# Where the adaptive norm's weight pieces stand in the two feed-forward blocks: 56 of 96 in the Down runs in place of 32

## The reference, cut to what matters

```
def _swiglu(h, w_gu, w_down):
    gate, up = jnp.split(h @ w_gu, 2, axis=-1)
    return (jax.nn.silu(gate) * up) @ w_down
...
    x = x + 0.5 * _swiglu(_rmsnorm(x, ffn1_norm), ffn1_w_gu, ffn1_w_down)
    x = x + _token_mixing(...)
    x = x + 0.5 * _swiglu(_rmsnorm(x, ffn2_norm), ffn2_w_gu, ffn2_w_down)
...
    c_act = jax.nn.silu(c)
    for l in range(2):
        mod = c_act @ w_ada[l] + b_ada[l]            # w_ada[l]: 2048 x 6144
        shift, scale, gate = jnp.split(mod, 3, axis=-1)
        h = _rmsnorm_2(x, norm_g[l]) * (1.0 + scale) + shift
```

## Time and profile before

| | us |
|---|---|
| median of 3 runs | 3013.56 |
| lowest, highest | 3011.37, 3015.36 |
| the profiled execution | 3013.77 |
| its span (first to last instruction) | 3012.0 |
| PE busy in it | 2990.2 |
| DVE, POOL, ACT busy | 2138.6, 1531.6, 1502.0 |
| first Down runs, PE's first matmul to the last | 490.85 to 730.7 |

### The profile page before, as it was taken

One profiled execution on the slowest core, in us unless ns is written; L12 is line 12 of the kernel. 1 busy time (PEld: TensorE's weight loads), 2 busy tenths in 40 slices (PEclk: granted clock), 3 DMA queues, 4 the chain that ended last, 5 costly groups with the idle time before them and its releaser, 6 DMA issues.

```text
span 3012.0 us, 48048 instructions
## 1 busy us (share of the span) xinstructions
PE 2990.2 (99%) x19120; PEld 2671.4 (89%) x19120; DVE 2138.6 (71%) x3446; ACT 1502.0 (50%) x1999; POOL 1531.6 (51%) x749
## 2 busy tenths in 40 slices
PE   8999999999999999999999999999999999999998
PEld 7888888888999999998888888888899998999997
DVE  4889886764324447787688887777579866789764
ACT  6555544444667455544555554444544454534454
POOL 5887764445565555585578876444550004710013
PEclk9999999999999999999999999999999999999999
DMA  6888887885776555566688888788576546666455
GB/s 217 288 278 271 278 280 247 305 288 181 229 176 176 158 165 148 151 171 201 200 284 282 266 281 287 242 306 277 173 216 194 162 147 216 181 190 182 154 182 181
DMA packets 491671, 663.43 MB, mean 220 GB/s; under 512 B 70440, under 2 KB 278040, under 8 KB 490936
## 3 DMA queue, kind: packets, MB, share of 16 engines
q1 hardware_dynamic: 485960, 655.85, 68.2%
q0 software_dynamic: 4448, 2.94, 0.4%
q10 hardware_dynamic: 1040, 1.58, 0.2%
HBM read 656.06 MB, written 2.11 MB: 219 GB/s over the span
## 4 chain that ended last, share of the span: by engine, by line
PE 95%; DVE 3%; ACT 1%; DMA 0%; issue 0%; POOL 0%; DVEq 0%; ACTq 0%
PE ps L1142 33%; PE ps L1006 20%; PE ps L1147 17%; PE ps L1012 10%; PE ps L1023 3%; PE ps L1175 2%; PE ps L1028 1%; PE ps L1171 1%; PE ps L990 1%; PE ps L1667 1%; DVE narrow_split_slabs L2261 1%; PE ps L1181 1%; PE ps L1443 1%; PE ps L1424 1%; PE ps L1178 1%; DVE h_split L2218 1%
## 5 line engine op out<-in xcount | busy, mean ns | idle before, releaser
L925 POOL TENSOR_TENSOR split_slabs<-stage,split_slabs 128x1024 fp32r<-128x1024 f32 x366 | 892.3, 2447 | 1005.4 <-ACT split_slabs L1723 999.4
L1723 ACT ACTIVATE split_slabs<-stage 128x1024 fp32r<-128x1024 f32 x544 | 573.4, 1059 | 558.3 <-PE ps L1147 435.8
L1723 ACT ACTIVATE narrow_split_slabs<-stage 128x1024 fp32r<-128x1024 f32 (+1 forms) x437 | 457.3, 1050 | 589.1 <-PE ps L1012 442.5
L1142 PE MATMUL ps<-split_slabs,h_split 128*128 128x512 f32 x2904 | 719.6, 390 | 0.8 <-ACT split_slabs L1723 0.8
L1142 PEld LDWEIGHTS ps<-split_slabs,h_split 128*128 128x128 f32 x2904 | 541.7, 188 | 111.4 <-ACT split_slabs L1723 1.2
L1006 PE MATMUL ps<-h_split,narrow_split_slabs 128*128 128x256 f32 x4928 | 620.6, 279 | 3.1 <-issue 1.9
L925 POOL TENSOR_TENSOR narrow_split_slabs<-stage,narrow_split_slabs 128x1024 fp32r<-128x1024 f32 (+1 forms) x182 | 441.2, 2434 | 315.8 <-ACT narrow_split_slabs L1723 315.5
L1006 PEld LDWEIGHTS ps<-h_split,narrow_split_slabs 128*128 128x128 f32 x4928 | 586.7, 188 | 13.0 <-issue 7.7
L2261 DVE TENSOR_TENSOR split_slabs<-stage,split_slabs 128x1024 fp32r<-128x1024 f32 x178 | 258.3, 1453 | 272.8 <-ACT split_slabs L1723 272.0
L2261 DVE TENSOR_TENSOR narrow_split_slabs<-stage,narrow_split_slabs 128x1024 fp32r<-128x1024 f32 x255 | 338.3, 1330 | 126.5 <-ACT narrow_split_slabs L1723 126.1
L1147 PE MATMUL ps<-split_slabs,h_split 128*128 128x512 f32 x1452 | 388.2, 389 | 0.0
(11 more groups left out here) (346 smaller groups left out, 3293.0 us busy)
## 6 DMA issues: line engine op xcount, KB each, us to landing
stage<-in_ffn_w_gu SPq DMA_DIRECT2D x352, 512.0 KB, 4.8
stage<-in_w_in SPq DMA_DIRECT2D x349, 512.0 KB, 3.7
U<-in_w_ada SPq DMA_DIRECT2D x192, 512.0 KB, 5.7
stage<-in_ffn_w_down SPq DMA_DIRECT2D x176, 512.0 KB, 5.2
stage<-in_w_out SPq DMA_DIRECT2D x96, 512.0 KB, 4.2
stage<-in_w_in SPq DMA_DIRECT2D x80, 128.0 KB, 2.9
stage<-in_w_branch_c SPq DMA_DIRECT2D x32, 192.0 KB, 3.4
stage<-in_cmp_w SPq DMA_DIRECT2D x8, 512.0 KB, 4.3
```

The costliest lines, as they stand in the source:

```text
L925: nc.gpsimd.tensor_tensor(slab_part(n, 1, size(n)), stage[:, n % RING, 0:size(n)], slab_part(n, 0, size(n)).bitcast(F32), ALU.subtract).th ...
L1142: mm(ps[:, 2 * pair + T, :], stationary(kk, i)[:, T * P:(T + 1) * P], w[0][:, kk, :], start=first and kk == 0 and i == 0, stop=False)
L1723: return fn(slab_part(n, 0, size(n)), stage[:, n % RING, 0:size(n)], ACT.Copy)
```

## The change

Of the 96 pieces of each block 40 stand in the gate and up run in place of 64, and 56 stand in Down in place of 32. In Down they stood at each odd slab from 9 to 71; now they stand at each slab from 9 to 71 that is not a multiple of 8. The first piece of all stays at slab 26 of the block and the last at Down's 71. From Down's slab 8 on, DVE keeps the low part of each fourth slab only (9, 13, 17, ... 85); 20 low parts of each block go from DVE to POOL, so that POOL has 65 of Down's 88 and DVE 23.

```diff
-ADA_EARLY = 64
+ADA_EARLY = 40
...
         by_vector |= set(summed)
+        by_vector -= {s + GU_SLABS + i for s in (S_F1, S_F2) for i in range(8, DOWN * DOWN_GROUPS) if i % 4 > 1}
```

## The result

The changed kernel takes 3086.71 us (median of 4 runs, 3081.34 to 3090.05), the kernel before 3014.3 beside it (3011.37 to 3015.36): a ratio of 1.0239, with a 95% interval of 1.0225 to 1.0253. It is 72.4 us slower; 45.6 were forecast. The profiled execution took 3090.05 us with a span of 3088.2, so it is the slowest of the four, 3.3 above the median.

The account below looks back on a forecast made before the run. PE was taken as the bound, busy 2990.2 of 3012.0 us. Fewer gate and up pieces 0, low parts to POOL 0, added Down pieces 2 x 22.8: 45.6 us on 3013.77, so 3060, range 3026 to 3092.

Parts of the forecast that it names:

- part 2: Down: moving 20 low parts a block from DVE to POOL costs 0, the longer latency covered by SP's spare.
- C(15): Down: end of DVE's taking of the piece at slab 15, forecast near 536 in the new trace.
- about 20 us: Down: PE idle expected per block in the new trace, ended by POOL's or ACT's slabs.
- the upper case of the prediction: Down: pieces land in 6.0 us, period 3.78 us a piece, stall 36 us a block, total 3086.
- Start of the walk: Down's slabs 9 to 15: DVE's activation transposes delay pieces, so slab 15's is taken 4.2 us after that slab starts.
- Period: Down: with two buffers, each piece takes half of landing 5.5 plus taking 1.54 plus 0.02, 3.53 us.
- the deadline: Down: slab k's piece must be taken by 0.4 us after slab k starts, or slab k+3's load is late.
- the norm work: Down from slab 22: DVE's norm transposes may hold pieces some us each group, up to about 3092; not in the sum.
- 1: Down: loads spread out and land in 4.6 us, so 0 to 3 us lost, 3014 to 3017; chance 0.09.
- 2: Down: DMA throughput limits, not the two buffers; 9 us a block, 3031; chance 0.13, shared with landings 4.7 to 5.0.
- 3: Gate and up runs: fewer pieces there relieve them and make the kernel faster; chance 0.02.
- rival 4: Down: PE's clock falls to 1.2 GHz in stalls, time above 3092; chance 0.08, shared with norm transposes in full.

Follow-up runs that it names:

- e5: Changed kernel with POOL making every low part of Down from slab 8 on, none left on DVE there: 3052.2 us.
- e9: 48 pieces in each Down as in e8, but each piece one slab later, so DVE's low-part slabs carry none: 3037.8 us.
- e12: Changed kernel with DVE's order turned at Down's slabs with a piece, the piece taken ahead of the low part: 3068.7 us.
- e1: Changed kernel with only the pieces moved; the low parts shared as before, DVE having each odd slab: 3089.2 us.
- e6: Changed kernel with DVE's four low parts of the next norm put one each at four slabs instead of in a row: 3078.2 us.
- e3: Changed kernel with a third piece buffer in the first block's Down, the second block keeping two: 3055.9 us.
- e8: Changed kernel with 48 pieces in each Down in place of 56: 3067.9 us.
- e10: Changed kernel with SP issuing each piece of Down two slab loads later in its order: 3101.6 us.
- e4: Changed kernel with 40 pieces in each Down in place of 56: 3014.6 us.

## Why the prediction was right in kind and 27 us short

**Bound, place and mechanism held.** No gain in the gate and up runs; part 2 cost nothing; PE's idle in Down ended mostly by ACT's and POOL's slabs (16.2 of 19.2 us in the first Down, the rest by DVE's); SP's wait over 100 us (149.2); 277 GB/s in 490 to 760 and 295 in 550 to 700, where 318 were forecast; the time inside 3026 to 3092. Of the signs named, C(15) was wrong in size, eight slabs took 26.3 us in place of 24.7 (mean of slabs 17 to 69), pieces landed in 5.0 and 4.7 us in the median, at and under the lower edge of "5 to 6", and the stall did not end at 72 but at 76.

**Where it was luck.** The 19.2 us meet the sign "about 20 us" only because the forecast took idle for the whole stall: the stall is 34.4. And the upper case of the prediction has almost the very period, stall and total that were measured (3.78, 36, 3086), but from a landing of 6.0 us, which didn't come; with the real landing of 5.0 its own formula gives 3.28 and a time near 3033. The range held the result since one term was put too high where another was too low.

**The sum, term by term**, first Down:
- Start of the walk: C(15) at T(15) + 4.2 forecast, 531.65 = T(15) + 1.64 measured. Pieces 11, 12 and 15 landed in 3.9 to 4.0 us, not 5.5. 22.8 becomes 20.2.
- Period: 3.53 forecast, 3.78 measured, 47 x 0.25 = 11.8 us more. This is the step that failed. Its two parts missed in opposite ways. The landing was 5.0 in the mean, not 5.5. But from landing to taken it was 2.60 us over the 56 pieces, where the prediction had 1.56 (1.54 + 0.02), as if DVE were free whenever a piece lands. So the term that failed is the wait for DVE, which the formula had at nothing; it measured 1.0 us a piece.
- At slab 69 PE was at C(69) - 2.0, where the deadline allowed 0.4: 1.6 less. Then 4.0 more at slabs 70 to 76, behind the last pieces.
- 20.2 + 11.8 - 1.6 + 4.0 = 34.4. The second Down, with 3.86, comes to 37.0; its norm step differs (`rest_raw`), and its pieces of slabs 26 to 35, not counting those behind a low part, waited 23.1 us beyond 1.57 each, the least that any piece takes from landing to taken, against 14.9.

**What DVE was doing.** e5 shows the first cause: without low parts of Down on DVE the period is 3.50 and 3.64, and the stalls fall by 15.8 and 14.3 us. By the loop it should be 14 slabs (17 to 69) x 1.05 = 14.7. That fit is better than the estimate deserves: in the first Down C(k) is within T(k) + 1.44 to 1.46 at five of the 14 slabs only, and at the others between 0.5 and 5.0, where the landing or the norm's work moves it. e9 shows the cause by position and e12 by order alone. That e1, with twice as many low parts on DVE, isn't slower than the changed kernel fits: one such slab in four is enough to tie the piece to T(k) + 1.4. The load that is held is that of slab k+3, so in both kernels k+4 is the next slab of DVE's that can add to the same delay (worked out from the order, not measured). The prediction had the deadline T(k) + 0.4, and in its walk of slab 13 it had the low part ahead of the piece; it didn't ask where C(k) must lie at such a slab once loads are late. The second cause, the norm work, it named as an end of its range and left out of the sum; e6 measures one part of it at 8.5 us (7.0 of stall). The upper end of 3092 was hardly enough.

**The rivals.** 1 (landing 4.6 or less, no loss) fell: the landing came down to 5.0 and 4.7 in the median, the latter at the very edge of its sign, but not the period. 2 (rate of transfers) fell with e3. 3 fell with rows 60 to 480. 4 came true in small measure, next section.

**Open.** How the norm's transposes, its low parts and the fold share the rest wasn't taken apart. Nor is it known how much of the half clock's 10 us lay on the path, since a slower PE is also waited for less. No version here beats the kernel before: its Down has 0.4 us of stall, so there is nothing for the pieces to win.

## What to carry to other kernels

A background stream that shares an in-order DMA queue with the main one has a period, (landing + wait for the consumer + taking) / buffers; and the wait for the consumer must be taken from the schedule in the late state, not from a kernel in which all is early. Look for a loop: if the consumer's queue holds main work ahead of the background item, and the next main load is queued behind that item's release, lateness feeds itself. Then the position of the items counts for more than their number (e8 and e9: 30 us by one slab), and moving one queue's order without the other's only moves the wait (e10).

## What the runs showed of the hardware

**PE's clock fell after short pauses, and in six runs once without one.** PE in the changed kernel around slab 36:

```profile
595.00:599.00 4.00, 3.58 (x15) 2.34 (x14) 3.57 (x5) 0.94 (x1) 2.40 (x1) 1.00 0.51 139
599.00:602.50 3.50, 0.67 (x3) 0.19 (x1) 1.51 (x2) 0.91 (x1) 0.00 (x0) 1.00 0.94 338
602.50:606.00 3.50, 3.31 (x8) 2.63 (x9) 2.69 (x4) 1.20 (x2) 0.34 (x1) 0.51 0.98 361
606.00:610.00 4.00, 4.00 (x20) 3.28 (x19) 1.74 (x3) 1.06 (x1) 3.68 (x2) 1.00 0.89 269
```

PE was busy for 0.67 of 3.5 us, then got half its clock (0.51, the 1.2 GHz level) for 3.4 us, in which eight matmuls took 3.58 us in place of 1.98, and then full clock again. The changed kernel has such falls at 602, 640, 2036, 2060 and 2677, about 10 us lost at most; the kernel before has none but in its last 10 us. In the 3.4 us before 640 PE was busy for 1.42. e10, where PE's waits are longest in sum (29.3 us in its first Down), has 26 us of it. Six of the runs (e3, e4, e5, e6, e8, e12) also have a fall at 845 to 876, between the two blocks, that no pause precedes. In e5, length, PE's busy time, clock, DMA share and GB/s:

```profile
859.80:863.20 3.40, 3.34 (x27) 0.99 0.41 84
863.20:866.60 3.40, 3.40 (x18) 0.50 0.89 185
```

PE was busy for 3.34 of 3.40 us, 2.2 of them with sixteen small matmuls of 30x30, and then had half its clock all the same. What set off this fall is open. The prediction's rival 4 had put this above 3092; it was a part of the loss below that.

**Landing times under load.** 512 KB landed in 3.9 us at the least and 5.0 in the median in the changed kernel's first Down (277 GB/s), and in 6.5 in the median with three buffers (342 GB/s). More transfers in flight gave more bytes a second although each took longer: 382 GB/s in e3's best 15 us, above the 366 of the earlier trace rows.
